# A hybrid mLSTM and attention decoder layer: the small products of an mLSTM step in two groups, not three

## The reference

```python
s = jnp.einsum('bhtd,bhsd->bhts', qc, kc) * w
num = w_int[..., None] * jnp.einsum('bhtd,bhde->bhte', qc, C) + jnp.einsum('bhts,bhse->bhte', s, vc)
den = w_int * jnp.einsum('bhtd,bhd->bht', qc, n) + jnp.sum(s, axis=-1)
h = num / jnp.maximum(jnp.abs(den), jnp.exp(-m_row))[..., None]
C_new = decay[..., None, None] * C + jnp.einsum('bhs,bhsd,bhse->bhde', wk, kc, vc)
n_new = decay[..., None] * n + jnp.einsum('bhs,bhsd->bhd', wk, kc)
```

## Time and profile before

| what | value |
|---|---|
| median of three executions | 1674.96 us (1674.1 to 1676.04) |
| the profiled execution | 1675.36 us |
| its span | 1673.6 us |
| TensorE busy | 1650.2 us, 99% of the span |
| VectorE busy | 952.3 us, 57% |
| ScalarE busy | 632.4 us, 38% |
| GpSimd busy | 350.9 us, 21% |
| share of TensorE in the chain that ended last | 96% |

### The profile page before, as it was taken

The page is one execution under the profiler, slowest core; times in us unless marked ns, Lnnn a source line. Parts: engine busy times, 40 slices in busy tenths (PEclk is TensorE's granted clock), DMA queues, the critical chain, the costliest instruction groups (busy, mean ns, idle before and its releaser), DMA issues.

```text
span 1673.6 us, 26868 instructions
## 1 busy us (share of the span) xinstructions
PE 1650.2 (99%) x10083; PEld 1497.7 (89%) x10083; DVE 952.3 (57%) x1745; ACT 632.4 (38%) x1403; POOL 350.9 (21%) x349
## 2 busy tenths in 40 slices
PE   8999999999999999999999999999999999999997
PEld 8999999899998899888978899999999999999996
DVE  5412333343135544674544877777777777767787
ACT  5523333232235423453302444333444443443432
POOL 2002001110001200121000233333333222333354
PEclk9999999999999999999999999999999999999999
DMA  7105355552311132311231011111101111111113
GB/s 218 52 26 136 61 72 99 52 85 29 71 29 26 26 83 45 60 27 26 63 132 51 26 51 51 50 50 50 48 27 50 50 50 50 50 35 40 50 63 114
DMA packets 138794, 99.47 MB, mean 59 GB/s; under 512 B 82376, under 2 KB 128464, under 8 KB 138712
## 3 DMA queue, kind: packets, MB, share of 16 engines
q1 hardware_dynamic: 138712, 98.34, 24.1%
HBM read 88.43 MB, written 11.60 MB: 60 GB/s over the span
## 4 chain that ended last, share of the span: by engine, by line
PE 96%; DVE 2%; DMA 1%; issue 1%; ACT 1%; POOL 0%; SPq 0%; DVEq 0%; POOLq 0%; ACTq 0%
PE bank L889 37%; PE bank L1237 23%; PE bank L1217 6%; PE bank L1270 6%; PE bank L1271 6%; PE bank L1269 6%; PE bank L845 3%; PE bank L1278 2%; PE bank L1074 2%; PE bank L1044 1%; PE bank L954 1%; PE bank L946 1%; PE bank L949 1%; PE bank L991 1%; PE bank L929 0%
## 5 line engine op out<-in xcount | busy, mean ns | idle before, releaser
L1237 PE MATMUL bank<-xT_hi,w_hi 128*128 128x384 f32 (+1 forms) x768 | 250.9, 327 | 1.0 <-DVE xT_lo L1814 1.0
L1237 PE MATMUL bank<-xT_hi,w_lo 128*128 128x384 f32 (+1 forms) x768 | 250.8, 327 | 0.0
L1237 PE MATMUL bank<-xT_lo,w_hi 128*128 128x384 f32 (+1 forms) x768 | 250.7, 326 | 0.0
L889 PE MATMUL bank<-xT_hi,w_hi 128*128 128x384 f32 (+1 forms) x1008 | 195.5, 335 | 0.0
L889 PE MATMUL bank<-xT_hi,w_lo 128*128 128x384 f32 (+1 forms) x1008 | 186.3, 326 | 0.0
L889 PE MATMUL bank<-xT_lo,w_hi 128*128 128x384 f32 (+1 forms) x1008 | 186.1, 326 | 0.0
L2494 POOL TENSOR_TENSOR e<-gain_b,e 128x512 f32<-128x512 f32 x60 | 78.0, 1301 | 435.4 <-ACT gain_b L1743 435.4
L889 PEld LDWEIGHTS bank<-xT_lo,w_hi 128*128 128x128 f32 x1008 | 168.7, 188 | 0.0
L889 PEld LDWEIGHTS bank<-xT_hi,w_lo 128*128 128x128 f32 x1008 | 168.7, 188 | 0.0
L889 PEld LDWEIGHTS bank<-xT_hi,w_hi 128*128 128x128 f32 x1008 | 166.1, 188 | 2.7 <-issue 1.0
L1789 DVE TENSOR_TENSOR w_lo<-raw,w_hi 128x1024 fp32r<-128x1024 f32 (+1 forms) x54 | 70.4, 1303 | 158.5 <-ACT w_hi L1382 158.3
(11 more groups left out here) (259 smaller groups left out, 3026.8 us busy)
## 6 DMA issues: line engine op xcount, KB each, us to landing
raw<-in_w_in SPq DMA_DIRECT2D x64, 256.0 KB, 4.5
raw<-in_w_up SPq DMA_DIRECT2D x16, 1024.0 KB, 5.4
raw<-in_w_down SPq DMA_DIRECT2D x16, 1024.0 KB, 5.0
raw<-in_w_in SPq DMA_DIRECT2D x9, 1024.0 KB, 5.8
xin<-in_x_prompt SPq DMA_DIRECT2D x8, 512.0 KB, 4.0
bc<-gate_rows SPq DMA_DIRECT2D x32, 128.0 KB, 6.0
Cin<-in_state_C SPq DMA_DIRECT2D x4, 1024.0 KB, 7.6
out<-Cin SPq DMA_DIRECT2D x16, 256.0 KB, 8.6
```

Source lines behind the costliest of these rows:

```text
L889: last = nc.tensor.matmul(out, lhsT, rhs, start=(step == 0), stop=(step == 3 * KT - 1))
L1237: last = nc.tensor.matmul(bank[unit_bank(g, u)][:, 0:cn], w[:, 0, k * WCOLS + tile * P:k * WCOLS + (tile + 1) * P], x[:, k, c0:c0 + cn], s ...
```

## The change

The transposes of the step before and the pair move ahead of the step's own products, into one group, and the two fill slots between them become one slot of two units. Since the pair now writes banks 4 and 5 shortly before the update products do, those wait for VectorE's sampled_states of that pair (ml_sc); and since the pair writes them after the scores, it waits until these are read (ml_kw, ml_sw). ScalarE copies the transposes out (ml_third) ahead of ml_second, and VectorE runs sampled_states ahead of ml_second, behind ml_exponents. The third step keeps its four slots and its pairs; only the transposes stand ahead of it.

```diff
--- before.py
+++ after.py
@@ -178,9 +178,9 @@
 W_P0, W_SS, W_P1 = [3] + [3] * 16, [8] + [4, 2] * NSEQ, [3] + [3] * 16
 ORDER = [0, 1, NT - 1] + list(range(2, NT - 1))
 SAMPLE_AT = ORDER.index(NT - 1)
-SLOTS = [[1, 1, 1] for _ in range(NT)]
+SLOTS = [[2, 1] for _ in range(NT)]
 SLOTS[SAMPLE_AT] = [1, 1, 1, 1]
-SLOTS[NT - 1] = [1, 1]
+SLOTS[NT - 1] = [2]
 
 
 def ml_fills(units, first):
@@ -950,6 +950,8 @@
                                                 start=False, stop=True)
                 last.then_inc(ml_n, 1)
                 pe.wait_ge(ml_kw, s + 1)
+                if pairs_before(s + 1):
+                    pe.wait_ge(ml_sc, pairs_before(s + 1))
                 for hh in range(2):
                     last = nc.tensor.matmul(bank[4 + hh][:, 0:VA], kw[0:n, s % 2, hh, :], vaug[p][0:n, i, hh, :],
                                             start=True, stop=True)
@@ -979,9 +981,12 @@
 
                 p, i = s // S_PER, NT - 1
                 hh, j = divmod(g, 4)
-                done = chunks_before(s + 1)
+                done = chunks_before(s)
                 if g == 0:
                     pe.wait_ge(ml_kz, p + 1)
+                if tile_of_step(s) != i:
+                    pe.wait_ge(ml_kw, s + 1)
+                    pe.wait_ge(ml_sw, s + 1)
                 if done:
                     pe.wait_ge(ml_c, done)
                 if PAIRS * p + g:
@@ -1014,17 +1019,18 @@
                 for x in range(NT):
                     s = s0 + x
                     pairs = pairs_in(x)
+                    if x:
+                        ml_transposes(s - 1)
                     if x == SAMPLE_AT:
                         ml_sampled(s)
                     else:
+                        if pairs:
+                            ml_pair(s, pairs[0])
                         ml_step(s)
                     fill(slots[x][0])
-                    if pairs:
+                    if x == SAMPLE_AT:
                         ml_pair(s, pairs[0])
-                    if x:
-                        ml_transposes(s - 1)
-                    fill(slots[x][1])
-                    if x == SAMPLE_AT:
+                        fill(slots[x][1])
                         ml_pair(s, pairs[1])
                         fill(slots[x][2])
                     if x + 1 < NT:
@@ -1532,12 +1538,12 @@
                     s = s0 + x
                     if x + 1 < NT:
                         ml_weights(s + 1)
+                    if x:
+                        ml_third(s - 1)
                     ml_second(s)
                     fill(slots[x][0])
-                    if x:
-                        ml_third(s - 1)
-                    fill(slots[x][1])
                     if x == SAMPLE_AT:
+                        fill(slots[x][1])
                         fill(slots[x][2])
                     if x + 1 < NT:
                         ml_keys(s + 1)
@@ -1951,13 +1957,14 @@
                     pairs = pairs_in(x)
                     if x + 1 < NT:
                         ml_exponents(s + 1)
+                    if pairs and x != SAMPLE_AT:
+                        sampled_states(p, pairs[0])
                     ml_second(s)
                     ml_norm(s)
                     fill(slots[x][0])
-                    if pairs:
+                    if x == SAMPLE_AT:
                         sampled_states(p, pairs[0])
-                    fill(slots[x][1])
-                    if x == SAMPLE_AT:
+                        fill(slots[x][1])
                         sampled_states(p, pairs[1])
                         fill(slots[x][2])
                     if x + 1 < NT:
```

## The result

The changed kernel takes **1680.32 us** (median of 8 runs, 1680.02 to 1680.65) against 1674.33 of the kernel before (8 runs, 1674.07 to 1676.04): 6.0 us more, a ratio of 1.0035 with a 95% interval of [1.0026, 1.0044]. Its profiled execution took 1680.11 us, with a span of 1678.4.

The account below looks back on a forecast made before the run. The prediction took TensorE's own order of products to set the mLSTM stretch's time. Ways out 0.6, added wait 8.4 and vanished waits -1.4 made +7.6 on 1675.36, 1683.0, adjusted to the median: 1682.5 us, range 1678.0 to 1686.0.

Parts of the forecast that it names:

- The added wait: Update products wait until VectorE has added the pair to the sampled states; eight stalls in 12 one-pair steps, +8.4 us.
- the last two kinds of step: One-pair steps preceded by one gating operation and exponents (1 step), or by neither split nor exponents (3): stall 0.
- the step worked out: From S, the last fill's end before a step: update products due S + 3.00, exponents end S + 3.42; stall 1.47 us.
- With nothing laid bare: By a skill rule on weight-load overlap, the eight stalls would lose 0.13 each, 7.4 in all; the prediction disagreed.
- Ways in and out: Entering the pair's 32-row products stays 0.10; leaving them for full products or fills costs 0.047 more, 14 times: +0.6 us.
- The waits that go: TensorE's old waits, 0.8 at the second half's last transposes and 0.4 at next-step scores, vanish with bare loads: -1.4 us.
- At nothing: Effects counted as zero, such as transposes preceding the norm with 8 us of cover, and the pair's new waits.
- The tight end: End of the second half, with one fill only, where last transposes await the norm: 0 to 0.8 once, taken as 0.
- Borders are what costs: Faster rival: the pair's going in and out, 3.2, and the 1.4 of waits vanish without stalls: 1670.4; chance 0.04.
- The new wait is hidden: Rival within 0.2%: VectorE adds the pair in time everywhere, leaving -0.8: 1674.2; chance 0.09.
- The clock falls: Rival: 1.5 us stalls inside a group of small products lower TensorE's clock, 13.6 at four long stalls: 1696; chance 0.04.
- Further chains turn late: Rival: the norm comes too late for the transposes, 0.9 in up to 8 steps: 1686 to 1690; chance 0.03.

Follow-up runs that it names:

- run 1: Changed kernel with VectorE adding the pair to the sampled states ahead of the next step's exponents, still behind the last fill's gating and split: 1677.70 us.
- run 2: Changed kernel with VectorE adding the pair to the sampled states ahead of the last fill's gating and split and the exponents: 1672.85 us.
- run 3: Changed kernel with the exponents (two VectorE operations) computed twice: 1685.74 us.
- Run 7: As run 2, with the pair ahead of the transposes in TensorE's merged group: 1672.91 us.
- run 6: Kernel before with the four transposes moved into the middle of the next projection unit, 26 more borders: 1675.07 us.
- run 8: As Run 7, with the pair of the very last step behind its fill on TensorE and VectorE: 1672.75 us.
- run 4: Kernel before with the exponents computed twice, as a control: 1675.03 us.
- run 5: Kernel before with only the transposes moved ahead of the step's products, the pair staying behind the first fill: 1675.28 us.

## Why the prediction was right, and where its sizes were off

The likeliest case came about: slower by more than 0.2%, with 6.0 us against the 7.6 forecast, 1680.3 inside the range of 1678.0 to 1686.0. Of the 2.2 between 1680.3 and the 1682.5 forecast, 0.6 is the kernel before, which the prediction took from three executions (1674.96) and which is 1674.33 over eight; the rest is sizes, as follows.

- **The added wait** was right in place, number and kind: eight stalls, none in the last two kinds of step. In size it was 8.0 instead of 8.4. Due time and VectorE's free time were exact in the step worked out (S + 3.00, S + 3.42); L1911 starts 0.09 before the exponents end, as put, and TensorE 0.15 after the end of L1911. What was too large is the weight load that stands bare after a wait: 0.13 taken, 0.07 measured. With nothing laid bare, which would have made 7.4, the four update products would take their 0.68 behind a wait too; they take 0.75 or 0.76 in all eight. Runs 1, 2 and 3 show the mechanism by taking it away in part, in whole, and by adding to it; in run 3 the stretch grew by the 4.4 of the sum.
- **Ways in and out.** The way in stayed as it was; out into a full product of the step was put at 0.13 and is 0.11, out into a transpose is 0.06. The difference, 0.05, is the 0.047 of the prediction. Run 7 took it away again and left about 0.4 for it, put at 0.6.
- **The waits that go**, 1.4: both went. By the start-to-start times of the kernel before they were worth 1.5.
- **At nothing.** The tight end was rightly 0 in the changed kernel, but only behind its last stall; run 2 laid it bare with 0.5. The border, 0.01 in 14 places and taken as nothing, was counted short: a merged group loses two borders, and 26 went, which by run 6 are worth some 0.3.
- **The sum.** 8.0 + 0.6 - 1.5 - 0.3 = 6.8 in the stretch, and 6.8 is measured; the 0.3 is an estimate from run 6, not a run of the changed kernel with its borders put back. The median grew by 6.0 only. The time behind the stretch is 0.5 to 0.6 shorter than before in the changed kernel and in runs 1, 2, 3, 7 and 8, but not in 4, 5 and 6: VectorE waits for the output DMA once, 0.7 us, instead of twice, 1.1, in the last 35 us, and the rest is not traced. No step of the prediction had this term, and no run tried it. So one sign that the prediction named for being right, nothing changed outside the mLSTM stretch, did not hold.
- **The rivals.** "Borders are what costs": run 6 refutes it, with 0.01 a border. "The new wait is hidden": made true by run 2, which gave -1.3, where the rival's price was -0.8. "The clock falls": it stayed at 1.00 through stalls of 1.4 us. "Further chains turn late": none did in the changed kernel, and the norm did once, in run 2. The drain that the Trainium skill (TensorEngine Tiling (Array Packing), Key Properties) states for a change of tiling mode agrees again with a cost of going into the 32-row products, now behind transposes: 0.09 (0.53 for the transposes ahead of the pair, of which 0.44 is their own). That this cost is a drain, no row shows.

## What to carry to other kernels

Before merging groups of small products, look in TensorE's start-to-start times for what a border costs; here a border between float32 and float32r products of full size cost 0.01 us, and only the 32-row products paid, 0.09 to 0.10 going in and 0.06 to 0.13 coming out. When two results share a bank within one group, the time between them must cover not the reader's work alone but all that stands ahead of this work in the reader's queue. List that queue at the moment of release, kind of step by kind of step. The remedy was on the reader: the same two lines moved up in VectorE's queue turned +6.0 us into -1.3, and the -1.3 is hardly to be told from no change.

## What the runs showed of the hardware beyond that

After a wait for VectorE's semaphore, the first full product of the changed kernel takes 0.07 us more than in a stream (0.29 instead of 0.216 to the next start), and its weight load starts only with it (337.93 against 337.96 in the step above); behind the 32-row products a product of the step takes 0.11 more (0.32). In the kernel before, TensorE's slack against VectorE was smaller than the page of its profile suggests: 0.65 us more in each step on an engine that is busy 38% of the stretch (104.77 of 275.00) cost 1.0 us.
